# Projecting the next tile's queries and values between the steps of the prompt's attention

## What is computed

```
z = h @ w_in;  zq, zk, zv, zu, zs = split(z)             # 5 columns of 512
q = zq.reshape(B, S, 8, 2, 32); k likewise; v = zv.reshape(B, S, 8, 64)
s = einsum('bqhjd,bkhjd->bjhqk', q * 32**-0.5, k) - slopes * dist   # causal
p = softmax(s);  a = p[:, 0] - lam * p[:, 1]             # two score maps per head
o = einsum('bhqk,bkhd->bqhd', a, v)                      # then RMS norm per head
```

## Time and profile before

| | us |
|---|---|
| median of 3 runs | 948.0 (947.82 to 953.27) |
| the profiled execution's own time | 947.89 |
| its span | 946.2 |
| TensorE busy | 841.9 (89%) |
| DVE, ACT, POOL busy | 346.4, 208.9, 118.8 |
| last group's turn ends to first score | 226.7 to 229.9 |
| prompt attention on TensorE | 229.9 to 327.8 |
| samples' attention starts | 336.0 |

### The profile page before, as it was taken

One profiled execution on the slowest core, in us unless ns is written; L12 is line 12 of the kernel. 1 busy time (PEld: TensorE's weight loads), 2 busy tenths in 40 slices (PEclk: granted clock), 3 DMA queues, 4 the chain that ended last, 5 costly groups with the idle time before them and its releaser, 6 DMA issues. The chain is left out here.

```text
span 946.2 us, 12198 instructions
## 1 busy us (share of the span) xinstructions
PE 841.9 (89%) x4720; PEld 436.2 (46%) x4720; DVE 346.4 (37%) x843; ACT 208.9 (22%) x436; POOL 118.8 (13%) x190
## 2 busy tenths in 40 slices
PE   4699999997789679999988999479999999999995
PEld 3244444333555455665654455344444444444431
DVE  2304332104778545555451364442103011101137
ACT  4001001103666324333330211110101111101122
POOL 1300000002200112222120010001000000000044
PEclk8899999999779879999998998669999999999998
DMA  8996203635910047999797951508888999999973
GB/s 312 365 306 246 89 17 112 259 147 183 410 42 1 1 164 285 413 417 428 298 367 263 340 217 34 200 23 354 335 340 325 401 425 401 396 428 381 409 281 119
DMA packets 36709, 249.15 MB, mean 263 GB/s; under 512 B 4377, under 2 KB 5785, under 8 KB 23218
## 3 DMA queue, kind: packets, MB, share of 16 engines
q1 hardware_dynamic: 22834, 155.17, 41.8%
q0 software_dynamic: 9376, 81.47, 22.0%
q10 hardware_dynamic: 4448, 11.82, 3.8%
HBM read 231.91 MB, written 16.53 MB: 263 GB/s over the span
## 5 line engine op out<-in xcount | busy, mean ns | idle before, releaser
L770 PE MATMUL ps<-sb 128*128 128x512 f32 x320 | 142.8, 602 | 1.8 <-DVE sb L410 1.8
L2054 PE MATMUL ps<-sb 128*128 128x512 f32 (+1 forms) x256 | 112.9, 594 | 0.0
L770 PEld LDWEIGHTS ps<-sb 128*128 128x128 f32 x320 | 60.1, 192 | 75.7 <-issue 74.0
L1206 PE MATMUL ps<-sb 128*128 128x128 f32 x512 | 66.1, 284 | 18.8 <-ACT sb L1075 9.3
L1206 PEld LDWEIGHTS ps<-sb 128*128 128x128 f32 x512 | 57.6, 145 | 32.4 <-issue 18.3
L1978 DVE TENSOR_TENSOR sb<-sb,ps 128x512 f32<-128x512 f32 (+1 forms) x16 | 10.9, 684 | 160.3 <-PE ps L2054 87.1
L2044 PE MATMUL ps<-sb 128*128 128x512 f32 x144 | 66.4, 616 | 1.0 <-ACT sb L1896 0.9
L2079 PE MATMUL ps<-sb 128*128 128x512 f32 x144 | 63.5, 594 | 0.0
L1726 PE MATMUL ps<-sb 128*128 128x512 f32 x128 | 58.4, 616 | 3.9 <-DVE sb L1485 3.9
L2054 PEld LDWEIGHTS ps<-sb 128*128 128x128 f32 (+1 forms) x256 | 42.0, 167 | 34.0 <-issue 34.0
L958 PE MATMUL ps<-sb 128*128 128x128 f32 (+3 forms) x128 | 50.1, 526 | 3.2 <-ACT sb L871 3.2
(11 more groups left out here) (297 smaller groups left out, 1018.6 us busy)
## 6 DMA issues: line engine op xcount, KB each, us to landing
sb<-in_w_gate SPq DMA_DIRECT2D x16, 2048.0 KB, 19.4
sb<-in_w_up SPq DMA_DIRECT2D x16, 2048.0 KB, 9.5
sb<-in_w_down SPq DMA_DIRECT2D x16, 2048.0 KB, 14.2
sb<-in_w_ada SPq DMA_DIRECT2D x12, 2048.0 KB, 15.5
sb<-in_w_in SPq DMA_DIRECT2D x5, 2048.0 KB, 24.6
y_rows<-sb SPq DMA_DIRECT2D x9, 512.0 KB, 15.5
sb<-in_w_out SPq DMA_DIRECT2D x2, 2048.0 KB, 21.2
sb<-in_x_prompt SPq DMA_DIRECT2D x4, 512.0 KB, 5.1
```

Of the source, the lines that this page charges most:

```text
L770: last = pe.matmul(PS[:, n % 4, :], L.hT[:, k, t * P:t * P + P], w[:, k, :], start=k == 0, stop=k == KC - 1)
L1206: last = pe.transpose(PS[:, h, P * g:P * g + P], kp[:, 4 * (ch % 2) + g, P * h:P * h + P], L.cst("ident"))
L2054: last = pe.matmul(PS[0:n, 1, :], x[:, k, :], w_up[:, k, :], start=k == 0, stop=k == KC - 1)
```

## The change

The groups (v, t) and (q, t) leave `project` and go into `attend_prompt`. (q, 0) and (v, 0) are formed ahead of step 0. Those of tile t = 1 to 4 are cut in quarters of two matmuls (for t = 4 of two half matmuls), and `beside(n)` puts one into a step of tile t - 1, two into its first, between the turned weights of step n - 2 and the values of step n - 3; in the fourth step the queries are turned instead. The ada rounds move to behind (s, 2) and (u, 1), their weights and those of v and q to other slots, the list of loads with them. Scores contract over the component's 32 rows straight from `qT` and `kT`; `place_q` is gone. DVE forms the bias minus the scores with a minimum, so that the negation (L938) is gone and ACT's exponential has scale -1 and waits for its own map alone. `finish` is spread over the third, fourth and fifth step of the next tile (`taken`, `squares`, `normed`); the values of all tiles use one PSUM bank. Page loads: three are issued behind the u groups and the last ada round, three in the last tile and behind its last values. The stores of v go from ACT to SP.

```diff
-ADA = [[0, 1, 2, 3], [3, 4, 5, 0], [3, 4, 5, 0]]
-WIN = [4, 5, 0, 1, 2]
+ADA = [[0, 1, 2, 3], [1, 2, 3, 4], [1, 2, 3, 4]]
+WIN = [4, 5, 0, 5, 2]
-ADA_AFTER = [("v", 2), ("q", 2)]
+ADA_AFTER = [("s", 2), ("u", 1)]
+def beside(n):
+    t, k = n // H + 1, n % H
+    if n >= 4 * H:
+        return []
+    return [[("q", t, 0), ("q", t, 1)], [("q", t, 2)], [("q", t, 3)], [("turn", t, 0)],
+            [("v", t, 0)], [("v", t, 1)], [("v", t, 2)], [("v", t, 3)]][k]
...
-            for i in range(4):
+            for i in range(3):
                 pool.wait_ge(ss_ready, i + 1)
                 self.power(pool, link, ss, H, P, 1.0 / DV, ss_power)
+            pool.wait_ge(grp_done, group_at("q", 4) + 1)
+            self.load_pages(pool, self.ck, 1, 0, K_SLOT[1][0], 3)
+            pool.wait_ge(grp_done, group_at("v", 4) + 1)
+            self.load_pages(pool, self.cv, 0, 1, V_SLOT[1], 4)
+            pool.wait_ge(pv_done, N)
+            self.load_pages(pool, self.ck, 1, 1, K_SLOT[1][1], 5)
...
-                        pe.matmul(PS[:, 2 * (n % 2) + j, 0:P * (i + 1)], qz[i % 2][:, h // 2, 2 * (h % 2) + j, :],
-                                  L.kT[:, h // 2, 0:P * (i + 1)], start=True, stop=True).then_inc(s_done, 1)
+                        r = 32 * (2 * (h % 2) + j)
+                        pe.matmul(PS[:, 2 * (n % 2) + j, 0:P * (i + 1)], L.qT[r:r + 32, h // 2, P * i:P * i + P],
+                                  L.kT[r:r + 32, h // 2, 0:P * (i + 1)], start=True, stop=True).then_inc(s_done, 1)
...
+                for c, t, part in beside(n):
+                    if c == "turn":
+                        turn(t)
+                    else:
+                        product(c, t, part)
                 if n >= 3:
...
                 if n >= 1:
                     weights(n - 1)
-                if n % H == 4 and n // H >= 1:
-                    finish(n // H - 1)
-            finish(3)
+                for c, t, part in beside(n):
+                    if c == "turn":
+                        turned(t)
+                    elif t == 4 and part == 3:
+                        summed(c)
+                if n < N and n >= H:
+                    if n % H == 2:
+                        taken(n // H - 1)
+                    if n % H == 3:
+                        squares(n // H - 1)
+                    if n % H == 4:
+                        normed(n // H - 1)
```

More of the change, by code:

```diff
@@ L712, in _ @@
                     link(dve.tensor_scalar_mul(self.gsub, self.gsub, 1.0 - LAM_INIT))
[L713 to L717, removed]
                 if (c, t) in ADA_AFTER:
@@ L896, in _ @@
                                    ACT.Copy).then_inc(at_done, 1)
+                for c, t, part in beside(n):
+                    if c != "turn" and part == 3:
+                        project(c, t)
         @block.vector
@@ L945, in _, with product @@
+                if n < N and n >= H:
[5 more added lines that the diff above has]
+                        normed(n // H - 1)
+            taken(3)
+            squares(3)
+            normed(3)
         @block.tensor
         def _(pe):
-            pe.wait_ge(self.evac_done, 5 * NT)
-            pe.wait_ge(self.post_ev, self.posts)
-            pe.wait_ge(self.mod_sb, 9)
+            def product(c, t, part):
+                number = WIN_ORDER.index(c)
+                w = L.ring[WIN[number]].rearrange("p (k n) -> p k n", k=KC)
+                bank = bank_of(c, t)
+                if part == 0:
+                    if t == 0:
+                        pe.wait_ge(self.ring_full[WIN[number]], 16 * fills("win", 0, number))
+                    else:
+                        pe.wait_ge(post_ev, 2 * NT + t + (c == "v"))
+                    if c == "q" and t >= 2:
+                        pe.wait_ge(evac_done, group_at("v", t - 1) + 1)
+                if t < 4:
+                    for k in (2 * part, 2 * part + 1):
+                        last = pe.matmul(PS[:, bank, :], L.hT[:, k, t * P:t * P + P], w[:, k, :],
+                                         start=k == 0, stop=k == KC - 1)
+                else:
+                    for c0, k in ((0, part), (NS, part + KC // 2)):
+                        last = pe.matmul(PS[c0:c0 + NS, bank, :], L.hT[:, k, SEQ:TOK], w[:, k, :],
+                                         start=part == 0, stop=part == KC // 2 - 1)
+                if part == 3:
+                    last.then_inc(grp_done, 1)
@@ new lines, in turn @@
+            def turn(t):
+                r = rows(t)
+                pe.wait_ge(evac_done, group_at("q", t) + 1)
+                for h in range(HP):
+                    last = pe.transpose(PS[:, 7, P * h:P * h + r], E[t % 2][0:r, P * h:P * h + P],
+                                        L.cst("ident", r)[:, 0:r])
+                last.then_inc(post_done, 1)
+            pe.wait_ge(self.mod_sb, 9)
+            for part in range(4):
+                product("q", 0, part)
+            for part in range(4):
+                product("v", 0, part)
@@ L950, in _ @@
+            turn(0)
             for n in range(N + 3):
```

196 lines of the change are left out of this document (116 added, 80 removed).

## The result

The changed kernel takes **909.3 us** (median of 4 runs, 906.39 to 911.25) beside 947.9 for the kernel before (4 runs, 947.17 to 953.27): a ratio of 0.958 [0.953, 0.963], 38.6 us less, where 35.1 less were forecast. In a later round of runs it took 911.4 (5 runs) beside 945.7 (11 runs), 0.962 [0.960, 0.964]. The profiled execution is the fastest of the four, 906.39 with a span of 904.7.

The account below looks back on a forecast made before the run. TensorE was taken to bound the 182.0 us from the first v group to the last prompt values; 149.7 - 15.6 + 2.8 + 10 = 146.9, so 35.1 less than 947.9: 913 us, range 903 to 931.

Parts of the forecast that it names:

- Bound and order: First v group to last prompt values: TensorE bounds it; quarters between steps remove most of 32.3 us idle and half clock.
- Waits: Idle time of TensorE that stays or comes in the stretch, from hand-over to drain: 10 us in sum.
- Fourth and fifth steps: Each tile's turn waits for ACT's evacuation, the next quarter for DVE's copy: 2.5 us over four tiles.
- DVE in the last tile: DVE needs 29 to 30 us in the last tile, TensorE 27.5: 2.5 us added.
- The drain: Behind the last score, with the sample tile's sum of halves in front of the last weights: 2.5 us.
- Norms in tiles 1 and 2: Waits from the spread norms in these two tiles: 1.5 us.
- Pieces: Cutting groups in quarters: 28 pieces each start with an exposed weight load, 0.1 us apiece, 2.8 us.
- Old steps: Attention steps at full clock before the change, by tile 1.37, 1.7, 2.48, 3.25 us, eight each: 70.4 us.
- Row groups: 32-row scores overlap on different row groups: a step's scores take half plus 0.13 us, saving 15.6 us.
- The barrier: Behind the last values: still 8.2 us, with nothing taken for the late page loads.
- The rival of row groups that do not overlap: Scores run one after the other, only the order's gain stays: 19.3 us less, 928.6; chance 0.18.
- The lost lead: Rival: TensorE waits each step for turned weights because DVE is held, quarters stand behind: 76 us more, 1024; chance 0.04.

Follow-up runs that it names:

- experiment 7: The change with the last page load moved from behind the last values to behind the barrier; 902.1 us (6 timed runs), 0.955 of the kernel before.
- experiment 8: The change with the wait for the stores of v moved from the barrier to the output stage, late page load left in place; 909.3 us.
- experiment 1: The change with scores contracted over all 128 rows again, masking left out; 917.8 us, 0.966 of the kernel before.
- experiments 2 to 6: 2: change, groups ahead, 939.0; 3: kernel before, only 32-row scores, 955.8; 4: 2 with full-row scores, 922.05; 5, 6: 2 plus full-row or 32-row filler, 935.8, 1006.0 us.
- experiments 9 and 10: Experiment 9, and as 10 the change with quarters in pairs, halves of a group in some steps and none in others; 913.9 us (one run).
- experiment 9: The change with the norm of the tile before done in one piece in the next tile's third step; 925.9 us (one run).

## Why the prediction was right, and where it was not

**Bound and order: right.** TensorE bounded the stretch and the quarters took its gaps: the weights of step n - 2 came in time in all but a few steps. The first score came at 174.3 (said: near 176), round 2 at 133.15 (near 133) without a wait, last-tile scores at 1.06 (1.0), a step of tile 0 at 2.67 (2.8) and of tile 2 at 3.71 (3.7), the clock at 1.00. The last values came at 283.1, not 292. The waits for L954's weights add up to 2.5 us and the one for ACT's evacuation to 1.0, far from the 12 that would have refuted the forecast; but three of them (0.39, 0.52, 0.33) stand outside the fourth and fifth steps and the drain, where it wanted none.

**The sum, term by term.** 146.9 were forecast for a stretch that, with 14.0 of ada rounds added to its 125.9, takes 139.9: 7.0 less.

- *Waits, 10 forecast, 5.0 measured.* Hand-over 0.94 (said 1). Fourth and fifth steps 1.32 (2.5). DVE in the last tile 1.13 (2.5): the waits at 270.07, 273.87 and 279.96. The drain 1.00 (2.5). Norms in tiles 1 and 2: 0.39 (1.5), one wait in tile 1's seventh step, behind the norm's last two instructions, ahead of which DVE stood 0.56 for POOL's power. Smaller gaps make the rest.
- *Pieces, 2.8 forecast.* 28 by 0.08 are 2.2.
- *Old steps, too dear by 5.2.* Tile 0's 1.37 was read from rows partly at the lower clock. Now a step of it without its quarter takes 2.67 - 1.81 = 0.86, which with full-row scores and no change of shape would be 0.93: 3.5 less over eight steps. Tiles 1 (1.58 for 1.7) and 2 (2.39 for 2.48) give 1.7 more in the same way.
- *Row groups, too cheap by 3.3.* Eight times (0.13 + 0.34 + 0.55 + 0.76) is 14.2, less 32 times 0.06 is 12.3, for 15.6.

Sum: -5.0 - 0.6 - 5.2 + 3.3 = -7.5, for the 7.0 measured. These are errors of size: the waits were put too high, and 3.5 of the old steps' 5.2 come from a price read off rows partly at the lower clock.

**The barrier: wrong.** "The barrier still 8.2 us" and "I take nothing" for the last page load failed. The load's copy and issue did fit, as argued: POOL's power ends 4.6 us after the last values, as before (4.4). What was left out is the transfer itself: the term for the last load was put at nothing and measured 4.4. POOL in the change (the load, then the power), with the gap's end at 297.48:

```profile
285.89 1.48 POOL L798 DMA_INDIRECT sb<-in_cache_k,ints  x1 [0.81 <-POOL ints L795]
287.44 0.20 POOL L813 TENSOR_SCALAR sb<-sb 128x8 f32<-128x8 f32 x1
287.72 1.68 POOL L814 TENSOR_TENSOR sb<-sb 128x8 f32<-128x8 f32 x1
```

POOL computes nothing after 289.40. What stands between that and the samples is seen in the windows (length, PE busy, granted clock, DMA share, GB/s), first of the change:

```profile
289.40:294.10 4.70, 0.00 (x0) 0.50 0.88 377
294.10:297.48 3.38, 0.00 (x1) 0.50 0.00 0
```

and then of experiment 7, where POOL's power ends at 290.39:

```profile
290.39:294.10 3.71, 0.00 (x0) 0.50 0.00 0
```

The transfers end at 294.1, and from there the samples take 3.4 us to start; without the load they take 3.7 from the end of POOL's power, and in the kernel before 3.8. In experiment 8, too, the samples start 3.3 us after the last transfer (296.1 to 299.42). Moving this one load takes the 4.4 away (12.65 to 8.18), moving the wait for the stores does not (12.56). So the load holds the barrier, and these times fit a barrier that is not passed before its transfer has ended. Which wait in the program does that is not shown.

**The rival of row groups that do not overlap: wrong, but not idle.** It had a chance of 0.18, and the rows of experiment 1 refute it. What neither it nor the forecast saw is that after a fall of the clock steps with 32-row scores do not bring it back: 13.0 us and a slower kernel unless full-row work stands in the same steps (experiments 2 to 6). "The clock should hold", I wrote, because waits would go. It did hold at 1.00, and no wait in the stretch is over 1.00 us; that the quarters would have brought it back is seen in experiments 9 and 10, where it fell and returned. Whether 32-row scores with neither long waits nor quarters would hold it, no run tests. The parts of the change were summed as if each had its price by itself, and these two have not: 10.5 for the quarters and -13.0 for the rows alone, 18.1 together.

**The lost lead: a real mechanism.** Without the spread norms it comes three times and costs 19.3 (experiment 9). With the norm spread over three steps, no wait for DVE is over 1.00: the change stays clear of it.

**What was luck.** The range held for the time, and "faster" had 0.94. That 38.6 lies so near the 35.1 is in part luck: the stretch gave 7.0 more than forecast and the barrier took 4.4 back, two errors that the forecast did not set against each other. And the forecast was right about the clock without knowing what full-row work does for it.

## What to carry to other kernels

When two parts of a change lean on the same engine, price them together and also each alone: the part that makes the matmuls smaller may only pay beside the part that adds full ones (here 10.5 and -13.0 alone, 18.1 together). Work cut in pieces and put where an engine in order would wait gains as long as what it waits for has a whole step of slack; spread the side work of the engine that supplies it. And ahead of a barrier or a stage's end, count transfers in flight, not only the instructions that issue them: here 4.4 us.

## What the runs showed of the hardware

- **Matmuls over 32 rows and the clock.** At the first scores, with the same wait of 1.87 us ahead of them, the granted clock fell to 0.50 in four kernels. With 32-row scores it stayed there for 75.3 us, with TensorE busy 73.95 of them (and 26.30 of 26.30 in their middle), and with more 32-row work for 153 us without a gap; with the same steps over 128 rows, or with one full-row matmul added a step, it was back within 7 us, and the mean is 0.96 in both. The Trainium skill (TensorE: Matmul & The Clock Gate, What's actually happening) says that the gate follows how busy the engine has been; by that the busy windows should have run at the upper level. These runs disagree with it where "busy" is what the profile shows.
- **Row groups overlap in pairs.** Two fp32 matmuls of 512 columns take 1.06 together (at the upper level) and 1.82 one after the other over 128 rows. The Trainium skill (TensorEngine Tiling, Key Properties) says that a change of tiling mode drains the engine; the trace agrees, at 0.06 us a step: 1.9 of 909 us.
- **A barrier behind a page load** took 12.4 to 13.1 us from the last values on with the load issued just ahead of it (nine kernels), and 8.18 to 8.21 without (four traces); in the four traces read for it the samples start 3.3 to 3.8 us after the last transfer or POOL's last instruction, whichever is later.
